# Windowed attention woven into the levels of a gated recurrence, one head and query block per level, in an encoder layer on one core

## The reference

```python
h = swiglu(rmsnorm(x, ffn1_pre_norm), w_gate, w_up, w_down)          # d_ff 2816
x = x + 0.5 * rmsnorm(h, ffn1_post_norm)
proj = rmsnorm(x, mix_pre_norm) @ w_in      # q 512, k 128, v 128, hq, hf_fwd, hf_bwd, hi, hg: 512 each
att = rmsnorm(windowed_gqa_sink(q, k, v, sink), attn_out_norm)       # 8 heads of 64, |i-j| <= 128
o_fwd = scan(q = sigmoid(hq), v = silu(hi), f = lb + (1 - lb) * sigmoid(hf_fwd))   # 4 heads of 128
o = rmsnorm(o_fwd + o_bwd, hg_out_norm) * silu(hg)                   # o_bwd: the same, reversed in time
x = x + rmsnorm(concat([att, o]) @ w_out, mix_post_norm)
x = x + 0.5 * rmsnorm(swiglu(rmsnorm(x, ffn2_pre_norm), ...), ffn2_post_norm)
```

## Time and profile before

| | us |
|---|---|
| timed runs | 1125.75, 1117.67, 1125.0; median 1125.0 |
| profiled execution | 1117.59, span 1115.8 |
| TensorE busy | 1070.1 (96%) |
| VectorE, ScalarE, GpSimd busy | 433.2, 349.5, 445.2 |
| mean granted TensorE clock | 0.971 of 2.4 GHz |

### The profile page before, as it was taken

How to read it: one execution, slowest core, us unless ns; L and a number is a source line. 1 busy time by engine, 2 the same in 40 slices (tenths; PEclk the granted TensorE clock), 3 DMA queues, 4 the chain that set the end, 5 groups by cost and what they waited for, 6 DMA issues and landing times.

```text
span 1115.8 us, 13287 instructions
## 1 busy us (share of the span) xinstructions
PE 1070.1 (96%) x5075; PEld 880.0 (79%) x5075; DVE 433.2 (39%) x615; ACT 349.5 (31%) x547; POOL 445.2 (40%) x275
## 2 busy tenths in 40 slices
PE   6999999999999999999996899879999999999998
PEld 5988888888888878788884576669888888888886
DVE  4443434433010624566573623463434343430103
ACT  5322222222132534343324334543222222221211
POOL 2544444444444456554443300033444444444440
PEclk9999999999999999999997599989999999999999
DMA  6333333333433243211212200013333333323211
GB/s 213 95 99 93 108 94 94 94 94 95 136 104 100 68 137 95 76 38 58 76 57 76 75 1 2 1 57 95 95 94 94 94 105 95 101 94 113 95 57 76
DMA packets 133371, 96.06 MB, mean 86 GB/s; under 512 B 11458, under 2 KB 116434, under 8 KB 133331
## 3 DMA queue, kind: packets, MB, share of 16 engines
q1 hardware_dynamic: 133008, 95.43, 28.4%
q10 hardware_dynamic: 322, 0.08, 0.0%
HBM read 93.41 MB, written 2.10 MB: 86 GB/s over the span
## 4 chain that ended last, share of the span: by engine, by line
PE 90%; ACT 4%; DVE 3%; issue 1%; DMA 1%; POOL 0%; ACTq 0%; DVEq 0%
PE ps L779 17%; PE ps L780 17%; PE ps L781 17%; PE ps L786 10%; PE ps L788 9%; PE ps L787 9%; PE ps L1055 2%; PE ps L947 2%; PE ps L1083 2%; PE ps L1067 1%; PE ps L980 1%; ACT JK L480 1%; DVE YB L1214 1%; PE ps L803 1%; ACT WH L458 1%
## 5 line engine op out<-in xcount | busy, mean ns | idle before, releaser
L387 POOL TENSOR_TENSOR WL<-raw,WH 128x1024 fp32r<-128x1024 f32 x132 | 317.9, 2410 | 501.2 <-ACT WH L458 501.2
L779 PE MATMUL ps<-XH,WH 128*128 128x512 f32 (+1 forms) x912 | 346.1, 380 | 0.1
L781 PE MATMUL ps<-XH,WL 128*128 128x512 f32 (+1 forms) x912 | 343.1, 376 | 0.0
L780 PE MATMUL ps<-XL,WH 128*128 128x512 f32 (+1 forms) x912 | 343.0, 376 | 0.0
L458 ACT ACTIVATE WH<-raw 128x1024 fp32r<-128x1024 f32 x162 | 171.0, 1056 | 342.0 <-PE ps L781 177.4
L781 PEld LDWEIGHTS ps<-XH,WL 128*128 128x128 f32 x912 | 173.3, 190 | 30.9
L779 PEld LDWEIGHTS ps<-XH,WH 128*128 128x128 f32 x912 | 173.7, 190 | 30.2 <-issue 0.5
L780 PEld LDWEIGHTS ps<-XL,WH 128*128 128x128 f32 x912 | 173.5, 190 | 29.7
L786 PE MATMUL ps<-WH,hh 128*128 128x512 f32 x352 | 137.1, 390 | 0.0
L788 PE MATMUL ps<-WL,hh 128*128 128x512 f32 x352 | 137.0, 389 | 0.0
L787 PE MATMUL ps<-WH,hl 128*128 128x512 f32 x352 | 136.9, 389 | 0.0
(11 more groups left out here) (136 smaller groups left out, 920.6 us busy)
## 6 DMA issues: line engine op xcount, KB each, us to landing
raw<-ffn_w_gate SPq DMA_DIRECT2D x44, 512.0 KB, 3.7
raw<-ffn_w_up SPq DMA_DIRECT2D x44, 512.0 KB, 3.7
raw<-ffn_w_down SPq DMA_DIRECT2D x44, 512.0 KB, 3.7
raw<-w_in SPq DMA_DIRECT2D x22, 512.0 KB, 3.7
raw<-w_out SPq DMA_DIRECT2D x8, 512.0 KB, 3.2
X<-x SPq DMA_DIRECT2D x4, 512.0 KB, 6.7
raw<-w_in SPq DMA_DIRECT2D x8, 256.0 KB, 3.1
out<-X SPq DMA_DIRECT2D x8, 256.0 KB, 2.0
```

Source lines behind the costliest of these rows:

```text
L387: pool.tensor_tensor(low, raw[:, s, :], high.bitcast(fp32), ALU.subtract).then_inc(lo_done, 1)
L779: nc.tensor.matmul(dst, WH[:, s, w], xh, start=first, stop=False)
L780: nc.tensor.matmul(dst, WH[:, s, w], xl, start=False, stop=False)
L781: return nc.tensor.matmul(dst, WL[:, s, w], xh, start=False, stop=last)
```

## The change

1. **Order of units.** Head 0, head 1, then k, v and all four q, head 2, head 3, then four narrow gate units (one head of hg each, 24 matmuls as before) in place of the wide ones. Two halves of a unit run ahead of the first score group.
2. **Beats.** `mixer_beats` replaces the schedule: a beat is one score group. `counts` says how many halves it takes: 16 in head 0, then 7, 7 and 6, none in g = 0 and in g = 8 to 10 of heads 1 and 2, none in g = 7 to 10 of head 3.
3. **Attention in the beats.** From beat 12 (head 1, g = 1) each beat gets one of the 32 items. The order on TensorE is score group, `att_score(i)`, the halves (or values), `att_turn(i-1)`, `att_values(i-2)`. Scores use bank 2 alone, transposes bank 3 alone, values bank 6. The shift is made per item, by one small operation (maximum times minus scale, then minimum with the negative sink) right after the maximum. S shrinks to three items.
4. **ScalarE** thus has exps and sigmoids (head gates, output gates) in turn, and three square roots in beat 36, without preloads.
5. **Decay tree to GpSimd**, all seven rows of a head after its gates are ready, in two buffers.
6. **Output gate and norm of the recurrence.** Per head: the square is taken from bank 7 at once, the scale is one broadcast multiply, the head is turned for all tokens (`turn_o`), and the gate, silu(hg) times the norm weight (now one value a partition, loaded as one row instead of a broadcast to 128 partitions), is multiplied in after the turn.
7. **Out projection** after the last beat, tiles alone, two banks per chunk (4-5, 2-3, 6-7, 4-5), chunks 0 and 1 interleaved behind the last items, attention's tiles first. Highs and lows go to all of XH and XL. y is scaled in its bank, and its normed rows are turned into the bank that y has left.

```diff
-    between = [[("k",), ("v",)], [("q", 0)], [("q", 1), ("q", 2), ("q", 3)]]
-    ...
-    return units + [("hg", 2 * k) for k in range(4)]
+    units += [("head", 1, t) for t in range(3)] + [("k",), ("v",)] + [("q", j) for j in range(G)]
+    for h in range(2, NH):
+        units += [("head", h, t) for t in range(3)]
+    return units + [("gate", h) for h in range(NH)]
...
+    counts = [(2, 1, 2, 1, 2, 1, 2, 1, 2, 1, 1), (0, 1, 1, 1, 1, 1, 1, 1, 0, 0, 0), (0, 1, 1, 1, 1, 1, 1, 1, 0, 0, 0),
+              (0, 1, 1, 1, 1, 1, 1, 0, 0, 0, 0)]
...
-            return ps[2 + h] if s == 2 else ps[(0 if h else 4) + c]
+            return ps[(4, 2, 6, 4)[c] + h] if s == 2 else ps[(0 if h else 4) + c]
...
+            def decay_tree(h):
...
+                for lv in range(7):
+                    if lv:
+                        pool.wait_ge(tree_grown, 7 * h + lv)
+                    g = whole_decay(h, lv).rearrange("p d (b s) -> p d b s", s=2)
+                    pool.tensor_tensor(whole_decay(h, lv + 1), g[:, :, :, 0], g[:, :, :, 1], ALU.mult).then_inc(tree_grown, 1)
...
-            act.dma_start(HGN[:, :], io["hgrn_out_norm"][0].partition_broadcast(P)).then_inc(const_in, 16)
+            act.dma_start(vec_rows[4 * NH:NV, :], io["hgrn_out_norm"]).then_inc(const_in, 16)
```

ScalarE's list in the beats (the new lines):

```diff
+            for k in range(BEATS):
+                h, g = divmod(k, 11)
+                i = item_at(k)
+                ahead(MIX + min(at + 3, MIX_UNITS + 3))
+                if g < 7:
+                    mix_keys(h, g)
+                elif g >= 8:
+                    copy_scores(h, g)
+                if att_item(i - 2) and i % 2:
+                    copy_odd(i - 2)
+                if att_item(i):
+                    exp(i)
+                if k == ROOT_BEAT:
+                    root_o(0, 3)
+                    root_att(0)
+                    root_att(1)
...
+                for what, n, *p in BEAT[k]:
+                    if what == "half" and p[0]:
+                        at = n + 1
+                        if MIXU[n][0] == "head":
+                            head_sigmoid(n)
+                        elif MIXU[n][0] == "gate":
+                            out_gate_sigmoid(n)
```

TensorE's:

```diff
+            def att_score(i):
...
+                if i:
+                    pe.wait_ge(s_max, i)
...
+            def att_turn(i):
...
+                pe.wait_ge(s_exp, i + 1)
+                if i:
+                    pe.wait_ge((pt_even, pt_odd)[(i - 1) % 2], copied_count(i - 1))
...
+            for k in range(BEATS):
+                i = item_at(k)
+                scores(*divmod(k, 11))
+                if att_item(i):
+                    att_score(i)
+                for what, n, *p in BEAT[k]:
+                    if what == "half":
+                        half_unit(n, p[0])
+                    elif what == "turn":
+                        turn_unit(n)
+                    else:
+                        values(n)
+                if att_item(i - 1):
+                    att_turn(i - 1)
+                if att_item(i - 2):
+                    att_values(i - 2)
...
+            values(NH - 1)
+            att_turn(ITEMS - 1)
+            out_tile(0, 0)
+            out_tile(0, 1)
+            att_values(ITEMS - 2)
+            turn_o(2)
+            out_tile(0, 2)
+            out_tile(0, 3)
+            att_values(ITEMS - 1)
+            turn_att(1)
+            out_tile(0, 4)
+            out_tile(0, 5)
+            turn_o(3)
+            for n in range(4):
+                out_tile(1, n)
+            out_tile(0, 6)
+            out_tile(0, 7)
+            turn_att(2)
+            for n in range(4, 8):
+                out_tile(1, n)
+            for n in range(8):
+                if n == 3:
+                    turn_att(3)
+                out_tile(2, n)
+            turn(2, 0)
+            for n in range(8):
+                if n == 4:
+                    turn(2, 1)
+                out_tile(3, n)
```

VectorE's list has, per beat, the level (`grow` without the tree, `take_level`), `copy_even(i-2)`, `att_max(i)`, the division of a finished block in beats 22, 30 and 38, scaling and attention norm in beats 37 to 39, then the copies and gates of the beat's unit. After the out tiles of a chunk:

```diff
+            take_y(0)
+            add_y(2, 0)
+            low_att(3)
+            normed(2, 0)
+            take_y(1)
+            add_y(2, 1)
+            normed(2, 1)
+            split_low(2, 0)
```

## The result

| | before | after |
|---|---|---|
| timed runs, median | 1123.83 (1117.67 to 1125.75, 4 runs) | 1084.17 (1081.80 to 1088.39, 4 runs) |
| span of the profiled execution | 1115.8 | 1082.7 |
| TensorE busy, idle | 1070.1, 45.7 | 1055.2, 27.5 |
| mean granted clock | 0.971 | 0.990 |

The ratio is 0.969, 95% interval 0.966 to 0.973: 40 us less in the medians, 33.1 in the profiled spans. The forecast was 1088 with a range of 1070 to 1110.

The account below looks back on a forecast made before the run. TensorE, busy 1070.1 of 1115.8 us, was taken as the bound, losing to idle time and low clock. Work 270.5 + thin beats 10.0 + output tiles 7.3 + clock 6 = 293.8 against 325.0; with the start, forecast 1088 us, range 1070 to 1110.

Parts of the forecast that it names:

- thin beats, head 1: Levels 8 to 10 of head 1, without projection matmuls: VectorE's row shows, 0.7 us over three beats.
- head 2, level 8: Late gate, then multiplies, copy, maximum and a division on VectorE: 3.3 us wait, 0.4 in the beat after.
- head 3, level 5: Levels 3 to 5 of head 3: scaling, attention norm and third division in VectorE's row cost 1.9 us.
- head 3, level 7 and after: Gate, multiplies, mask and copy at level 7 cost 3.0 us, and 0.7 up to the head's end.
- chunk 3's first tile: Output tiles: chunk 3 takes back chunk 0's banks after its turn and split, 2.8 us wait.
- last chunk into the FFN: The last output chunk's way into the FFN stays, with two waits of 2 us before: 4.5 us.
- clock: Four waits of 2.8 us and more, each with 1.7 us lost to low clock behind it: 6 us, bounds 0 and 20.
- start: Kernel start: one row replaces the output norm's broadcast that TensorE's first turns wait for; gains 1 us, bounds 0 to 1.8.
- rival (a): The clock falls in the thin beats; if half of some 40 us is at half clock, +20, 1107 us; 15%.
- 270.5 of work: TensorE's work in recurrence, attention, output tiles and first FFN units at full clock: 270.5 us against 325.0 before.
- (b): Single banks for scores and transposes make items wait for the item before: 1 us per beat, +32, 1120 us; 8%.
- (c): ScalarE falls behind in full beats and TensorE's transposes wait for the exp; slower, past 1136 us; 6%.

Follow-up runs that it names:

- e2: The changed kernel with one half unit of head 2's output gate work moved from behind level 1 to behind level 8: 1077.33 us.
- e8: The changed kernel with three moves (a half unit each of heads 2 and 3 to later levels, chunk 3's transposes ahead of chunk 2's tiles): 1072.54 us, ratio 0.960.
- e3: The changed kernel with chunk 3's transposes issued ahead of chunk 2's out tiles: 1086.33 us.
- e9: The changed kernel with the half units of heads 2 and 3 moved as in e8, without the earlier transposes of chunk 3: 1075.29 us, ratio 0.961.
- e5: The changed kernel with the attention's exponentials taken as sigmoids (computes something else), 10 table loads instead of 31: 1085.26 us, ratio 0.971.
- e12: e8 with a one-column sigmoid ahead of every exponential, 72 table loads against 30: 1094.09 us, ratio 0.978.
- e11: e8 with a one-column sigmoid ahead of every second exponential, 54 table loads against 30: 1094.96 us, ratio 0.977.
- e1: The changed kernel unaltered, run again as yardstick: 1088.98 us, ratio 0.974 to the kernel before.
- e6: The changed kernel with only the weave undone, the 32 attention items alone after the recurrence's 44 beats: 1132.18 us, ratio 1.013 to the kernel before.
- e4: The changed kernel with the decay tree's products back on VectorE instead of GpSimd: 1089.72 us.
- e10: e8 with the decay tree's products back on VectorE instead of GpSimd: 1074.08 us, ratio 0.959.

## Why the prediction came out right

**The sum, term by term.** From the mixer's first norm to the last norm the change saved 29.3 us (before 385.55 to 753.83, after 383.39 to 722.39), where the prediction has 31.2:

| term | predicted | measured |
|---|---|---|
| thin beats, head 1 | 0.7 | 0.6 |
| head 2, level 8 | 3.3 + 0.4 | 3.5 + 0 |
| head 3, level 5 | 1.9 | 1.9 |
| head 3, level 7 and after | 3.0 + 0.7 | 1.5 + 0.9 |
| chunk 3's first tile | 2.8 | 2.4 |
| last chunk into the FFN | 4.5 | 1.2 |
| clock | 6 | 10.1 |
| start | 1 | 2.2 |
| waits in full beats | 0 | 0 |

**Waits.** All seven were named by place, five of them within half a us, and the five larger ones by engine too; head 1's (0.43 and 0.21) and the two behind level 7 (0.43 each) were for ScalarE's copy (L762), where the prediction had VectorE's row. Too high were two. At level 7 of head 3 the step that failed is the table load of 1.28 us that was put on the gate's way. ScalarE did it while it waited for the unit's matmuls, so the product ended 1.4 us behind the last of them, not 2.7:

```profile
640.51 1.28 ACT L715 ACT_TABLE_LOAD   x1
643.32 0.60 ACT L715 ACTIVATE SQX<-ps 128x512 f32<-128x512 f32 x1 [1.52 <-PE ps L875]
...
643.95 0.75 DVE L1505 SCALAR_TENSOR_TENSOR W<-ps,vecs,SQX 128x512 f32<-128x512 f32 x1 [3.49 <-ACT SQX L715]
```

The multiplies there took 0.68 us, not 0.87. At head 2's level 8 the product also ended early (0.9 us after the beat's start instead of 1.7), but the multiplies took 1.20 each, and the two errors cancel: that 3.3 met 3.5 is in part luck.

```profile
583.89 1.20 DVE L1456 TENSOR_TENSOR W<-W,GT 128x512 f32<-128x512 f32 x1 [0.31 <-PE ps L1044]
...
645.22 0.68 DVE L1461 TENSOR_TENSOR W<-W,SQ 128x512 f32<-128x512 f32 x1
```

So the mean of the earlier trace rows hides unlike durations. In after's beats the 30 of these multiplies with no GpSimd operation beside them took 0.68 or 0.69 us each; the 34 with one beside took 0.68 to 1.79, fourteen of them 0.95 or more. And the last chunk's way into the FFN was read off before, two waits of 2 us: one wait of 1.16 is left. The pair of operations that took 3.68 us before takes 1.42 here, with GpSimd idle (the window 716 to 726 has it at 0.00):

```profile
720.50 1.42 DVE L1326 SCALAR_TENSOR_TENSOR YB<-X,stats,GQ 128x512 f32<-128x512 f32 x2
```

The sum for the output tiles, 3.6, thus lies under the bound of 4. With it went a clock drop that the prediction had not seen: the first 46 us of FFN 2 had 0.96 before and 1.00 after, 1.7 us.

**Clock.** The mechanism was right (waits of some us in thin beats, a low stretch behind), the size was the term that failed: 6 predicted, with one drop of 1.7 us as the measure for all. The windows give 16 x 0.32 + 12 x 0.28 + 78.39 x 0.02 = 5.1 + 3.4 + 1.6 = 10.1. The drop of the earlier trace rows at 699 is the size of the smallest only; the one behind head 2 lasts 10 or 20 us. Nor are the places the predicted four: two of those had a drop (head 2's level 8, chunk 3's first tile), level 7 and the way into the FFN had none, and level 5 of head 3, with a predicted wait of 1.9 us that wasn't counted, had one. So rival (a) is true in kind and half in size. e2 and e8 bear the cause out: with head 2's wait closed levels 8 to 10 run at 1.00. They don't give a rule, since like waits had a low stretch in one execution and none in another (e3, e9).

**Work.** By the terms above, 22.1 against 23.3 us, the gain between the norms should have been 1 us over the forecast; it is 1.9 under it. Some 3 us are more than the 270.5 of work. They show in the full beats, which the prediction put at 4.9 and 5.5 us; a beat with a two-block item, then one with three blocks:

```profile
512.64:517.82 5.18, 5.18 (x30) 4.14 (x30) 2.93 (x7) 5.08 (x7) 3.75 (x4) 1.00 0.00 0
565.60:571.28 5.68, 5.68 (x34) 4.47 (x33) 2.88 (x7) 3.19 (x7) 0.38 (x1) 1.00 0.27 97
```

Fourteen such beats (five from 502.38, seven from 542.84, two from 605.66 on) are together 3.1 us over the forecast of 3.67 plus the item. But 3.67 is one of the shorter beats of before, where they go up to 4.02, so part of the 3.1 may be in the 165.9 already; what makes the beats longer stays open. The start (2.2, outside its bounds of 0 to 1.8; 1.4 of it is there at the first transposes of FFN 1) and the FFN's 1.7 make up for it: 33.1 measured, 32 predicted. That the total came so close is luck in part: the clock cost 4 us more and the work 3 us more than predicted, the waits 5 us less, and the start and the FFN gave 3 us more.

**ScalarE.** 17 more loads were predicted and 17 came (the terms that the prediction lists add up to 22 loads, not to its 24), hidden in full beats: e5 takes them out, and -20 us doesn't come. Rivals (b) and (c) fall with the first window: 0.9 us idle in 157.4. The Trainium skill (ScalarE: Activation LUTs, section What ACT_TABLE_LOAD costs) puts 2.66 us on a switch, load and drain; in this case only the load shows, also where nothing could hide a drain, as on ScalarE in e12:

```profile
562.63 0.20 ACT L533 ACTIVATE extra<-eps 128x1 f32<-128x1 f32 x1
562.84 1.28 ACT L751 ACT_TABLE_LOAD   x1
564.13 0.62 ACT L751 ACTIVATE S<-S,small 128x384 f32<-128x384 f32 x1
```

The same page of the Trainium skill, section Table sets: the hidden batching unit, says to finish one set before switching, which would have spoken against the change. With 17 loads more the full beats lost nothing; with 24 and 42 more on top (e11, e12) about 20 us were lost, and there the advice holds. Where between the two it begins to hold isn't shown.

**The size of the whole.** The page of after bears out the first step, that half clock and idle time bound the stage before: 14.9 us of busy time and 18.2 of idle time are gone, of the 26.6 (17.9 and 8.7) and 26.2 that the earlier trace rows put up. The median fell by more than the profiled span since the kernel before ran its timed runs above its profiled one, as the prediction allowed for in part. In e1's group the medians are 30.7 us apart.

## What to carry to other kernels

Ask of each idle stretch of TensorE not only how long it is but what the clock does behind it: here 3.5 us of waiting cost another 5 us or more, and moving one half unit of matmuls there took nearly all of both away. Work with long engine chains per item is best laid between matmuls that need nothing from it; the other engine's extra work (17 table loads) cost nothing in the full beats, where it fits, so count it against the beat as it will be, not as it is. To judge edits of 1 to 3 us, first remove the wait behind which the clock falls, since the runs spread by 7.6 us with it and by about 1 without (e2, e8); and look in the trace where the clock fell before a difference is put down to the edit (e9).

## What the runs showed of the hardware

- In a stretch of attention items alone the clock stayed at 0.50 over 40 us, though TensorE was busy for 38.7 of them (e6), as in the earlier trace rows.
- Like waits gave low stretches of 10 us in one execution and 20 in another (after and e3). The wait of 2.4 us ahead of chunk 3's first tile had a low stretch behind it in after, and none in e4 and e9. One of 1.62 us had one in e9, and none in e8. What decides isn't shown.
- A 128x512 multiply on VectorE (L1456, L1461 of after) took 0.68 or 0.69 us in all 30 cases with no GpSimd operation beside it. In 34 with one beside it took 0.68 to 1.79, in fourteen of them 0.95 or more, so no slow one was without a neighbour, but a neighbour alone doesn't decide. That GpSimd causes it wasn't tested by itself (in e10, with 14.2 us less on GpSimd, the time hardly moved).
- A table load took 1.283 us in every one of the 72 of e12, with no gap of more than 0.02 us ahead of it or behind it in the rows above.
